# A hybrid block (S5, HGRN2, differential attention, mixture of experts): the out-projection as three products of rounded parts and remainders

## The reference

```python
h = concat([meta, x])                                # 1040 rows x 1024
proj = rms_norm(h, norm_mix_g) @ w_in                # u | hq hf hi hg | aq ak av
y_ssm = s5_mixer(u, ...)                             # 256 columns
y_rec = hgrn2_mixer(hq, hf, hi, hg, ...)             # 256 columns
y_att = diff_attention(aq, ak, av, ...)              # 512 columns, 4 heads, two softmaxes each
mixed = concat([y_ssm, y_rec, y_att])                # 1024 columns
h = h + mixed @ w_out                                # the out-projection (w_out is 1024 x 1024)
h = h + hier_moe(rms_norm(h, norm_ffn_g), ...)       # router, 16 experts, top 2
return rms_norm(h, final_norm_g)[:, 16:]
```

## Time and profile before

| | |
|---|---|
| median of 3 runs | 1225.52 us (1220.72 to 1226.25) |
| the profiled execution | 1220.99 us, its span 1219.0 us |
| PE busy | 1089.6 us (89% of the span) |
| DVE, ACT, POOL busy | 836.6, 624.5, 455.7 us |
| out-projection, PE L1755 | 256 records, 464.3 to 691.9 us |

### The profile page before, as it was taken

One profiled execution on the slowest core, in us unless ns is written; L12 is line 12 of the kernel. 1 busy time (PEld: TensorE's weight loads), 2 busy tenths in 40 slices (PEclk: granted clock), 3 DMA queues, 4 the chain that ended last, 5 costly groups with the idle time before them and its releaser, 6 DMA issues. The chain is left out here.

```text
span 1219.0 us, 21718 instructions
## 1 busy us (share of the span) xinstructions
PE 1089.6 (89%) x6998; PEld 868.5 (71%) x6998; DVE 836.6 (69%) x1210; ACT 624.5 (51%) x984; POOL 455.7 (37%) x295
## 2 busy tenths in 40 slices
PE   5899899999978989999999738999999999999994
PEld 4898898989967555555555426878777787878873
DVE  4797847564377554544433287888887899898897
ACT  5522211177332454444333226777776787877863
POOL 1130211131001101111111114878776696877960
PEclk9999999999978999999999959999999999999998
DMA  7216434332053350011111684688999868877443
GB/s 261 85 39 75 121 86 133 95 105 70 20 99 96 141 194 1 35 52 47 45 65 52 235 300 156 216 270 297 322 374 365 292 224 275 258 258 215 111 157 155
DMA packets 89476, 194.95 MB, mean 160 GB/s; under 512 B 9248, under 2 KB 32032, under 8 KB 88752
## 3 DMA queue, kind: packets, MB, share of 16 engines
q1 hardware_dynamic: 82784, 169.91, 41.0%
q0 software_dynamic: 6624, 24.12, 8.4%
HBM read 220.60 MB, written 31.51 MB: 207 GB/s over the span
## 5 line engine op out<-in xcount | busy, mean ns | idle before, releaser
L2177 PE MATMUL ps<-split 128*128 128x512 f32 x1728 | 417.9, 397 | 21.4 <-DVE split L2275 13.2
L2177 PEld LDWEIGHTS ps<-split 128*128 128x128 f32 x1728 | 321.2, 190 | 99.9 <-DVE split L2275 21.0
L2223 ACT CAST split<-weights 128x1024 fp32r (+1 forms) x288 | 297.8, 1052 | 109.2 <-PE ps L2177 94.4
L2275 DVE TENSOR_TENSOR split<-weights,split 128x1024 fp32r<-128x1024 f32 x216 | 303.3, 1458 | 50.5 <-ACT split L2223 49.4
L464 PE MATMUL ps<-xsplit,wsplit 128*128 128x384 f32 (+2 forms) x1440 | 242.0, 326 | 2.7 <-POOL wsplit L236 2.7
L2120 POOL TENSOR_TENSOR split<-weights,split 128x1024 fp32r<-128x1024 f32 x72 | 197.7, 2745 | 106.4 <-ACT split L2223 105.6
L464 PEld LDWEIGHTS ps<-xsplit,wsplit 128*128 128x128 f32 x1440 | 228.6, 191 | 4.0 <-POOL wsplit L236 3.2
L236 POOL TENSOR_TENSOR wsplit<-mem,wsplit 128x1024 fp32r<-128x1024 f32 x22 | 57.3, 2605 | 249.4 <-ACT wsplit L319 249.4
L1755 PE MATMUL ps<-mem 128*128 128x512 f32 x256 | 116.9, 600 | 5.4 <-DVE mem L1581 5.1
L1553 DVE TENSOR_REDUCE sml<-ps 128x1 f32<-128x1040 f32 (+7 forms) x64 | 46.6, 769 | 80.5 <-PE ps L1700 80.5
L1637 ACT COPY mem<-ps 128x512 f32<-128x512 f32 (+3 forms) x48 | 21.4, 481 | 139.5 <-PE ps L1717 90.7
(11 more groups left out here) (413 smaller groups left out, 1420.5 us busy)
## 6 DMA issues: line engine op xcount, KB each, us to landing
weights<-in_w_down SPq DMA_DIRECT2D x26, 2048.0 KB, 16.3
weights<-in_w_gate SPq DMA_DIRECT2D x50, 1024.0 KB
weights<-in_w_up SPq DMA_DIRECT2D x50, 1024.0 KB
mem<-in_w_in SPq DMA_DIRECT2D x22, 512.0 KB, 4.4
mem<-in_x SPq DMA_DIRECT2D x10, 512.0 KB, 3.6
mem<-in_w_out SPq DMA_DIRECT2D x1, 4096.0 KB, 13.2
h_d<-mem SPq DMA_DIRECT2D x8, 512.0 KB, 2.6
xn_d<-mem SPq DMA_DIRECT2D x8, 512.0 KB, 2.6
```

The lines of the kernel that those rows point to most:

```text
L2177: mm = nc.tensor.matmul(ps[:, bank + h, :], x, w[place % RING][:, 512 * h:512 * h + 512], start=(k == 0 and p_ == 0), stop=(k == n - 1 and ...
L2223: nc.scalar.copy(WH[place % RING], raw(kind, k, q)).then_inc(wh_ready, 1)
L2275: nc.vector.tensor_tensor(WL[place % RING], raw(kind, k, q), WH[place % RING].bitcast(F32), ALU.subtract).then_inc(wl_dve, 1)
```

## The change

The out-projection is computed as in the experts. Each float32 matmul becomes three fp32r matmuls into the same bank: XH WH, XH WL, XL WH, where XH and WH are rounded copies and XL and WL the exact remainders. So a quarter has 12 matmuls instead of four. New names: `wo_high(k)` is WH of row k, `WOL_T[k]` its WL, MHIE and MLOE the two parts of the early rows (k < 4) of one tile, MHIL and MLOL those of the late rows.

- ACT rounds the weights, eight casts of 128 x 1024, at the end of steps 1 to 5 (`WO_AT`), each waiting for the weights' transfer.
- POOL makes the eight remainders at the head of `pool_attention`, ahead of all that it does there but a memset; each waits for its cast.
- ACT rounds the early rows of tile p with two casts of 128 x 256 at the end of step 4p+4 (`act_early_mix`); DVE makes their remainders in step 4p+4, behind the maxima (`dve_early_mix`). The late rows are rounded by the evacuation of `m` itself, and DVE makes their remainder from PSUM in step 4p+8 (`dve_late_mix`).
- PE waits for these (`xlo_ready`, `wlo_ready`), and the ring slot of `m` also for DVE.
- In a step that has both, the ring's `s` now comes ahead of `m`.
- SP issues the transfer of the weights without waiting for `glu_done`.

The diff, cut:

```diff
-            ring += [("s", p, None) for p in range(NT) if step_of("s", p) == step]
+            ring += [("s", p, None) for p in range(NT - 1) if step_of("s", p) == step]
...
+            ring += [("s", p, None) for p in (NT - 1,) if step_of("s", p) == step]
...
         def sp_attention(sp):
             sp.wait_ge(o_done, 16)
-            sp.wait_ge(glu_done, 8)
             sp.dma_start(WO, a["w_out"].rearrange("(k p) n -> p k n", p=P)).then_inc(late_loaded, 16)
...
         def pool_attention(pool, link):
             link(nc.gpsimd.memset(HALF, -0.5))
+            for k in range(WSPLIT0, KD):
+                pool.wait_ge(whi_ready, wo_split(k))
+                nc.gpsimd.tensor_tensor(WOL_T[k][:, :].rearrange("p (h n) -> p h n", h=2), WO[:, k].rearrange("p (h n) -> p h n", h=2),
+                                        wo_high(k).bitcast(F32), ALU.subtract).then_inc(wlo_ready, 1)
             pool.wait_ge(params_loaded, 80)
...
                 if 1 <= n <= NJOB:
                     dve_combine(dve, link, n - 1)
+                if n >= 8 and n % 4 == 0 and (n - 8) // 4 < NT:
+                    dve_late_mix(dve, (n - 8) // 4)
...
                     dve_maximum(dve, n, 1)
                 if n == 1:
                     dve_s5_gated(dve, 1)
+                if n >= 4 and n % 4 == 0 and (n - 4) // 4 < NT:
+                    dve_early_mix(dve, (n - 4) // 4)
...
+                for k in WO_AT.get(n, ()):
+                    act.wait_ge(late_loaded, 32)
+                    if k == 0:
+                        act.wait_ge(s5_done, 2)
+                    nc.scalar.copy(wo_high(k), WO[:, k].rearrange("p (h n) -> p h n", h=2)).then_inc(whi_ready, 1)
+                if EARLY_SPLIT and 4 <= n and n % 4 == 0 and (n - 4) // 4 < NT:
+                    act_early_mix(act, (n - 4) // 4)
...
+        WO_AT = {1: (0,), 2: (1, 2), 3: (3, 4), 4: (5,), 5: (6, 7)}
+        def act_early_mix(act, p):
+            if p:
+                act.wait_ge(early_used, p)
+            for i in range(2):
+                x, ks = early_halves(p, i)
+                ins = nc.scalar.copy(MHIE[:, ks], x)
+            ins.then_inc(xhi_ready, 1)
+        def dve_early_mix(dve, p):
+            dve.wait_ge(xhi_ready, X_DONE + p + 1)
+            for i in range(2):
+                x, ks = early_halves(p, i)
+                ins = nc.vector.tensor_tensor(MLOE[:, ks], x, MHIE[:, ks].bitcast(F32), ALU.subtract)
+            ins.then_inc(xlo_ready, 1)
+        def dve_late_mix(dve, p):
+            r, t = mix_at[p] - 1, tile_of(p)
+            dve.wait_ge(ring_free, r + 1)
+            nc.vector.tensor_tensor(MLOL[:, p % 2], slot(r).rearrange("p (h q) -> p h q", h=4), MHIL[:, :, P * t:P * t + P].bitcast(F32), ALU.subtract).then_inc(xlo_ready, 1)
...
-                mm = nc.tensor.matmul(ps[:, 2 + 3 * h, :], mix(k)[:, P * t:P * t + P], WO[:, k, 512 * h:512 * h + 512],
-                                      start=(k == 0), stop=(k == KD - 1))
+                o, wl = ps[:, 2 + 3 * h, :], WOL_T[k][:, 512 * h:512 * h + 512]
...
+                x, lo = (MHIE[:, k], MLOE[:, k]) if k < 4 else (MHIL[:, k - 4, P * t:P * t + P], MLOL[:, p % 2, k - 4])
+                nc.tensor.matmul(o, x, wo_high(k)[:, h], start=(k == 0), stop=False)
+                nc.tensor.matmul(o, x, wl, start=False, stop=False)
+                mm = nc.tensor.matmul(o, lo, wo_high(k)[:, h], start=False, stop=(k == KD - 1))
```

More of the change, by code:

```diff
@@ L115, in sem @@
             return ctx.enter_context(nc.semaphore(name))
+        with nc.sbuf_tensor("con_split", [P, C_END], F32R) as con_split_tensor:
+            con_split = con_split_tensor
         con = ctx.enter_context(nc.sbuf_tensor("con", [P, C_END], F32))
+        with nc.sbuf_tensor("par_split", [P, P_END], F32R) as par_split_tensor:
+            par_split = par_split_tensor
         par = ctx.enter_context(nc.sbuf_tensor("par", [P, P_END], F32))
@@ L128, in build, with split_at @@
             xsplit, wsplit = xsplit_tensor, wsplit_tensor
+        def split_at(name, off, n):
+            with ExitStack() as below:
+                if off:
+                    below.enter_context(nc.sbuf_tensor("below_" + name, [P, off], F32))
+                return below.enter_context(nc.sbuf_tensor(name, [P, n], F32R))
+        MHIE_T, HIL_T = split_at("mix_early", 0, 4 * P), split_at("mix_late", O_X + 4 * L, 4 * X)
+        MLOE_T = split_at("mix_early_lower", MEM - 512, 512)
+        WOL_T = [split_at("wo_lower%d" % k, O_C + 2 * KD * FF + 1024 * k, 1024) for k in range(KD)]
+        WOH_T = [split_at("wo_higher%d" % k, 9 * 1024 + L * k if k < 2 else 1024 * (2 * k - 7), 1024 if k < 2 else 2048)
+                 for k in (0, 1, 4, 5, 6, 7)]
         mem = ctx.enter_context(nc.sbuf_tensor("mem", [P, MEM], F32))
@@ L612, in build @@
         late_loaded = sem("late_loaded")
+        early_used = sem("early_used")
         UNITS = [(0, 3), (3, 6), (6, 8), (8, 11), (11, 14), (14, 16)]
@@ L1399, in outputs @@
                 mm.then_inc(o_done, 1)
+        EARLY_SPLIT = True
         oS = oC
@@ L1409, in build @@
         oS = oC + 2 * KD * FF
+        oWO = oS
         WO = take(KD, 1024)
@@ L1413, in build, with wo_high, wo_split, late_split @@
         RPART, FOLD = take(P), take(32)
+        assert oS <= MEM - 512
+        MLOE = MLOE_T[:, :].rearrange("p (k q) -> p k q", k=4)
         assert oS <= MEM
+        MHIE = MHIE_T[:, :].rearrange("p (k q) -> p k q", k=4)
+        MLOL = par_split[:, P_B1:P_END].rearrange("p (b h q) -> p b h q", b=2, h=4)
+        MHIL = HIL_T[:, :].rearrange("p (h t) -> p h t", h=4)
+        assert oAQ == O_X + 4 * L and oWO == O_C + 2 * KD * FF
+        def wo_high(k):
+            if 2 <= k < 4:
+                return con_split[:, C_COS + 1024 * (k - 2):C_COS + 1024 * (k - 1)].rearrange("p (h n) -> p h n", h=2)
+            return WOH_T[k if k < 2 else k - 2][:, :].rearrange("p (h n) -> p h n", h=2)[:, :, 0:512]
+        WSPLIT0 = 0 if EARLY_SPLIT else 4
+        W_DONE, X_DONE = 2 * NS, 18
+        def wo_split(k):
+            return W_DONE + k - WSPLIT0 + 1
+        def late_split(p):
+            return X_DONE + (2 * p + 2 if EARLY_SPLIT else p + 1)
+        def early_split(p):
+            return X_DONE + 2 * p + 1
         MASKB, IDENTB = (con[:, C_MASK + 64 * i:C_MASK + 64 * i + 64].bitcast(BF16) for i in range(2))
@@ L1652, in act_ring @@
                 t = tile_of(n)
-                nc.scalar.copy(AQ[:, :, P * t:P * t + P], b.rearrange("p (h q) -> p h q", h=4)).then_inc(ring_free, 1)
+                nc.scalar.copy(MHIL[:, :, P * t:P * t + P], b.rearrange("p (h q) -> p h q", h=4)).then_inc(ring_free, 1)
             elif kind == "x":
@@ L1708, in pe_ring @@
                 pe.wait_ge(ring_free, r - 1)
+                if ring[r - 2][0] == "m":
+                    pe.wait_ge(xlo_ready, late_split(ring[r - 2][1]))
             b = slot(r)
@@ L1751, in pe_out_quarter @@
                     pe.wait_ge(h1_ready, p)
+                if EARLY_SPLIT:
+                    pe.wait_ge(xlo_ready, early_split(p))
+                    pe.wait_ge(wlo_ready, wo_split(3))
             if q == 2:
                 pe.wait_ge(ring_free, mix_at[p])
+                pe.wait_ge(xlo_ready, late_split(p))
+                pe.wait_ge(wlo_ready, wo_split(KD - 1))
             for k in range(4 * late, 4 * late + 4):
-                mm = nc.tensor.matmul(ps[:, 2 + 3 * h, :], mix(k)[:, P * t:P * t + P], WO[:, k, 512 * h:512 * h + 512],
-                                      start=(k == 0), stop=(k == KD - 1))
+                o, wl = ps[:, 2 + 3 * h, :], WOL_T[k][:, 512 * h:512 * h + 512]
+                if k < WSPLIT0:
+                    nc.tensor.matmul(o, mix(k)[:, P * t:P * t + P], WO[:, k, 512 * h:512 * h + 512], start=(k == 0), stop=False)
+                    continue
+                x, lo = (MHIE[:, k], MLOE[:, k]) if k < 4 else (MHIL[:, k - 4, P * t:P * t + P], MLOL[:, p % 2, k - 4])
+                nc.tensor.matmul(o, x, wo_high(k)[:, h], start=(k == 0), stop=False)
+                nc.tensor.matmul(o, x, wl, start=False, stop=False)
+                mm = nc.tensor.matmul(o, lo, wo_high(k)[:, h], start=False, stop=(k == KD - 1))
+            if q == 1:
+                mm.then_inc(early_used, 1)
             if q == 3:
```

3 lines of the change are left out of this document (added).

## The result

The changed kernel takes 1204.0 us (median of 4 runs, 1201.95 to 1209.28) where the kernel before, run beside it, took 1225.53 (4 runs, 1220.72 to 1226.25): a ratio of 0.984, 95% interval 0.9804 to 0.9876, so 15 to 24 us less. The forecast was 1206, its range 1197 to 1217. The profiled execution took 1209.28 us, the slowest of the four; its span is 1207.5.

The account below looks back on a forecast made before the run. PE was taken to bound attention from 464 us on. Gain 24.6 minus costs 4.2, 1, 0.25, 0.5 and 1.4 gives 17.3 us less: 1203.7 from the profiled execution, 1208.2 from the median, middle 1206, range 1197 to 1217.

Parts of the forecast that it names:

- 32 quarters at the experts' pace: Out-projection on PE: twelve fp32r matmuls at 0.23 us replace four float32 ones, 0.77 us less per quarter, 24.6 in all.
- step 4, the combine late: Attention's step 4: POOL's weight remainder holds up DVE's early remainders, so the combine of job 4 ends 4.2 us later.
- the clock behind it: Behind step 4's stall: PE's idle time lowers the granted clock, costing 1 us, bounds 0 and 3.3.
- the casts of step 5: ACT in step 5: two weight casts of 2.1 us exceed its 1.87 us of idle time, costing 0.25 us.
- step 6, POOL's queue: POOL's small parameter operations and means' products behind the last remainder hold up the combine of job 6: 0.5 us.
- ring order: PE's ring: with `s` first, `m` waits for the `o` evacuation, 0.28 us in each of five steps, 1.4 us.
- later early remainders: Steps 8, 12, ... 32: early casts and remainders delay the combine by 1.5 us, within slack: cost nothing, bounds 0 and 3.
- the transfer: Weights' transfer, issued earlier, lands some 10 us ahead of its first cast: cost nothing, up to 2 us if attention inputs delayed.
- No stall: Rival: ACT and DVE finish step 4's early parts in time, no stall or clock loss, 1201 us; chance 0.13.
- POOL in steps 2, 3 and 5: Rival: POOL's remainders also hold up those steps' combines, 2.4 us each, plus one clock loss, 1215 us; chance 0.17.
- Handed back: Rival: the combine becomes late in most steps, so PE's gain is lost, 1219 to 1226 us; chance 0.06.
- Another pace: Rival: exposed weight loads make each out-projection matmul take 0.397 us, 39 us more instead of 24.6 less, 1270 us; chance 0.04.

Follow-up runs that it names:

- e2: Changed kernel with DVE's early remainders one step later, behind the combine of step 5: 1201.5 us, ratio 0.982 to the kernel before.
- e5: Changed kernel with SP again waiting for all the gate's matmul groups before issuing the weights' transfer: 1208.6 us, ratio 0.989 to the kernel before.
- e6: Changed kernel without the product of rounded rows and weights' remainder, 8 matmuls a quarter instead of 12: 1175.9 us, ratio 0.962 to the kernel before.
- e9: Changed kernel with early remainders one step later, `m` ahead of `s`, and quarters paired in every second step: 1220.3 us, ratio 0.998 to the kernel before.
- e3: Changed kernel with no weight cast in step 4, the eight spread over steps 1, 2, 3 and 5: 1202.3 us, ratio 0.983 to the kernel before.
- e1: Changed kernel with ACT's early-row casts ahead of the weight casts: 1200.6 us, ratio 0.983 to the kernel before.
- e10: Changed kernel run and traced once more, nothing altered: 1202.9 us, ratio 0.982 to the kernel before.
- e12: Kernel before, profiled once more, nothing altered: 1219.1 us, ratio 0.998 to the same kernel's other runs.

## Why the prediction was right, point by point

The time lies in the range and near the forecast, the stall came as described, and the gain on PE came out a fifth below the forecast. That 1204.0 us came out so close to 1206 is in part luck. Attention gave 14.9 us where 17.3 were forecast, which alone would lead from 1225.5 to 1210.6. The other 6.6 us arose outside attention, where the prediction counted nothing, and no run explains them (see "What is open").

| step | forecast, us | measured, us |
|---|---|---|
| 32 quarters at the experts' pace | -24.6 | 92.1 - 112.1 = -19.9 |
| step 4, the combine late | +4.2 | +3.8 (4.33 - 0.56, and 4.11 - 0.33 at PE) |
| the clock behind it | +1 | +1.0 |
| the casts of step 5 | +0.25 | 0 (the next evacuation starts 0.67 us behind PE's transposes, 0.66 before) |
| step 6, POOL's queue | +0.5 | 0 |
| ring order | +1.4 | +0.8 |
| later early remainders | 0 | 0 (e2) |
| the transfer | 0 | 0; 6 if it came late (e5) |
| sum | -17.3 | -14.3 (attention: -14.9) |

**The pace** is the term that was mis-sized, by 4.7 us. I took 0.229 us, read from 48 matmuls in a row, for a block of 12. Inside a quarter the pace is 0.233, and the first matmul adds 0.10; together 2.88 us for the 2.76 forecast, 3.8 us over 32 quarters. e6 gives the same fixed part with eight matmuls, and e9 shows that it is paid once for a block. The run of 48 has it too, but there it is spread over 48. The other 0.9 us: the 3.53 that I read in one quarter is at the upper end of what quarters took before (3.43 to 3.54), the mean is 3.50. That PE bounds the stage is shown by e6. Of the 0.6 us by which the sum misses the stage, 0.5 is PE's wait at the early quarters, 4.6 us now where it was 5.1. (The profile names DVE's residual as the releaser before and none now; it is the same place in the program.)

**Step 4** went as written, with its mechanism: POOL's remainder is released ahead of DVE's, DVE stands until POOL ends, and the combine behind it is late. e3 (POOL out of the way), e2 (the remainders behind the combine) and e1 (the hold moved to the combine) each change what it should change. The Trainium skill (SBUF — State Buffer, Who interferes with whom) says that the one that started first keeps the port to its end. The runs agree in both directions, except for the near tie of 0.03 us named at e1: a combine of 3.17 us in e1 where POOL was first by 0.13 us, a remainder of 2.93 us on POOL in e2 where DVE was first.

**The clock**: from the late transposes to the next mask row (L1695 before, L1780 now) PE took 470.98 - 466.12 = 4.86 us, and 458.61 - 454.79 = 3.82 before. These 1.0 us are the clock's: granted were 0.66 and 1.00. e2 and e3, with waits of 0.33 and 1.53 us, show no slow matmul there; e1, with 3.53, does (3.37 us for 2.05).

**Step 5 and 6**: POOL's last two remainders run from 473.13 to 477.83 and do hold DVE up, but not a combine (see the last section), and PE did not wait. My 0.5 us stood on the wrong operation.

**The ring**: `m` waits for an evacuation in five steps, as said, at 0.16 us a step and not 0.28. Whichever is second starts 1.10 us behind the first, before (608.73 - 607.63) and now (610.63 - 609.53); what changes is that `m` follows with 0.41 us to the quarter (611.04 - 610.63) where `s` did with 0.25. I had 0.53 for `m`.

**The rivals.** No stall: out, 4.11 us. POOL in steps 2, 3 and 5: out. In step 3 POOL is released at 454.82 behind the running combine, which takes 1.30 us, and PE's transposes wait 0.46 us there, as they did. Handed back: out for this change, in at e9. Another pace: out.

**What is open.** What makes the first matmul of a block dearer is open (see e9). The medians differ by 21.5 us (19.4 in the rounds of e10), attention by 15. The trace of the changed kernel lost 7.6 us ahead of attention and gained 4.2 behind it, against the first trace of before. The time ahead follows the clock granted in HGRN2: its products (L1368 before, L1385 now) took 54.9 us at 0.81 before and 57.1 at 0.76 in e12, 59.5 at 0.77 in the changed kernel, and from 55.0 at 0.82 (e6) to 61.0 at 0.73 (e2) in the variants, all with the same instructions. Behind attention both traces of before are at the slow end (521.8 and 527.2 us, the variants 514.7 to 522.0), with more idle time of PE ahead of the experts' products. The page's rows of before, before again, and the changed kernel twice, in this order:

```profile
L2177 PE MATMUL ps<-split 128*128 128x512 f32 x1728 | 417.9, 397 | 21.4 <-DVE split L2275 13.2
```

```profile
L2177 PE MATMUL ps<-split 128*128 128x512 f32 x1728 | 418.6, 398 | 26.1 <-DVE split L2275 18.3
```

```profile
L2277 PE MATMUL ps<-split 128*128 128x512 f32 x1728 | 416.6, 397 | 18.5 <-DVE split L2375 10.7
```

```profile
L2277 PE MATMUL ps<-split 128*128 128x512 f32 x1728 | 415.8, 397 | 16.1 <-DVE split L2375 7.7
```

Two traces against twelve can't tell a real gain of some 5 us there, which I had put at nothing, from chance; no run was made to part the two.

## What to carry to other kernels

Read the price of a matmul from a block as long as the one that you will have: the pace of a long run dilutes what the first matmul of a block costs, here up to 0.10 us in each of 32 blocks. Ahead of adding work to an engine that feeds the bound one, look at its queue: DVE's remainders, 0.8 us of work behind a wait for ACT's casts, cost PE 1.2 us ahead of the combine (e3), 3.8 with POOL's remainder and the weight cast beside them, and nothing behind it (e2). And spread the bound engine's work evenly over the steps of a pipeline: the same 384 matmuls in every second step cost all of the gain.
